# A layer stack on one core: where the attention outputs are turned, and how the branch products are cut

## The reference, cut to what matters

```python
y_fox = forgetting_attention(q_f, k_f, v_f, cum_logf).reshape(B, S, FOX_W)      # 8 heads, 512 wide
y_dsa = indexer_sparse_attention(q_d, k_d, v_d, q_i, k_i, w_i, rel_bias)        # 8 heads, 512 wide
merged = (jax.nn.sigmoid(gate_fox) * (y_fox @ w_branch_fox)
          + jax.nn.sigmoid(gate_dsa) * (y_dsa @ w_branch_dsa))
x = x + gate1 * (merged @ w_out)
```

## Time and profile before

| | |
|---|---|
| median of 3 runs | 1379.53 us (1378.36 to 1380.99) |
| profiled execution | 1380.45 us, span 1378.7 us |
| PE busy | 1329.7 us, 96% |
| PE weight loads | 1095.1 us, 79% |
| DVE busy | 824.6 us, 60% |
| ACT busy | 657.1 us, 48% |
| mean granted PE clock | 0.997 of full speed |

### The profile page before, as it was taken

One profiled execution on the slowest core, in us unless ns is written; L12 is line 12 of the kernel. 1 busy time (PEld: TensorE's weight loads), 2 busy tenths in 40 slices (PEclk: granted clock), 3 DMA queues, 4 the chain that ended last, 5 costly groups with the idle time before them and its releaser, 6 DMA issues.

```text
span 1378.7 us, 16276 instructions
## 1 busy us (share of the span) xinstructions
PE 1329.7 (96%) x6233; PEld 1095.1 (79%) x6233; DVE 824.6 (60%) x1119; ACT 657.1 (48%) x1048; POOL 79.9 (6%) x116
## 2 busy tenths in 40 slices
PE   2999999999999999999999999999999999999997
PEld 2788877788888788888877888887888888888885
DVE  5686767868465654457447554556553575755454
ACT  2666655553444543345655444444443444544342
POOL 3501100100000100001001000001000010100000
PEclk9999999999999999999999999999999999999999
DMA  9767654458455655654625754647556555564551
GB/s 336 252 201 250 233 206 173 163 183 316 142 196 170 214 184 197 195 187 172 207 111 161 218 193 161 202 164 229 183 201 196 184 194 203 184 213 184 172 203 52
DMA packets 156716, 268.37 MB, mean 195 GB/s; under 512 B 9477, under 2 KB 101717, under 8 KB 155616
## 3 DMA queue, kind: packets, MB, share of 16 engines
q1 hardware_dynamic: 148896, 239.43, 50.9%
q0 software_dynamic: 7744, 27.91, 6.0%
HBM read 266.21 MB, written 1.07 MB: 194 GB/s over the span
## 4 chain that ended last, share of the span: by engine, by line
PE 84%; DVE 5%; DMA 4%; ACT 3%; POOL 1%; issue 1%; SPq 0%; DVEq 0%; ACTq 0%; POOLq 0%
PE UP L685 16%; PE UP L687 16%; PE UP L686 16%; PE Y L685 9%; PE Y L687 9%; PE Y L686 9%; PE TB L759 3%; DVE WL L1449 2%; DMA RAW<-in_ffn_w_gu 2%; DMA RAW<-in_w_in 1%; DMA X<-in_x 1%; ACT WH L1088 1%; POOL RS L610 1%; PE Y L791 1%; POOL VAR L609 1%
## 5 line engine op out<-in xcount | busy, mean ns | idle before, releaser
L1449 DVE TENSOR_TENSOR WL<-RAW,WH 128x1024 fp32r<-128x1024 f32 (+1 forms) x442 | 507.8, 1194 | 186.0 <-ACT WH L1088 180.1
L1088 ACT CAST WH<-RAW 128x1024 fp32r<-128x1024 f32 (+1 forms) x442 | 429.9, 1032 | 220.1 <-PE Y L687 121.3
L685 PE MATMUL UP<-WH,AH 128*128 128x512 f32 (+1 forms) x1136 | 458.7, 404 | 5.1 <-DVE WL L1449 4.3
L687 PE MATMUL UP<-WH,AL 128*128 128x512 f32 (+1 forms) x1136 | 443.8, 391 | 0.0
L686 PE MATMUL UP<-WL,AH 128*128 128x512 f32 (+1 forms) x1136 | 442.6, 390 | 0.0
L685 PEld LDWEIGHTS UP<-WH,AH 128*128 128x128 f32 x1136 | 214.3, 189 | 49.6 <-issue 8.2
L687 PEld LDWEIGHTS UP<-WH,AL 128*128 128x128 f32 x1136 | 214.0, 188 | 45.3
L686 PEld LDWEIGHTS UP<-WL,AH 128*128 128x128 f32 x1136 | 214.7, 189 | 40.1 <-issue 0.2
L685 PE MATMUL Y<-WH,HH 128*128 128x512 f32 (+1 forms) x496 | 193.6, 390 | 0.0
L687 PE MATMUL Y<-WH,HL 128*128 128x512 f32 (+1 forms) x496 | 191.6, 386 | 0.0
L686 PE MATMUL Y<-WL,HH 128*128 128x512 f32 (+1 forms) x496 | 191.4, 386 | 0.0
(11 more groups left out here) (228 smaller groups left out, 932.8 us busy)
## 6 DMA issues: line engine op xcount, KB each, us to landing
RAW<-in_ffn_w_gu SPq DMA_DIRECT2D x176, 512.0 KB, 5.0
RAW<-in_ffn_w_down SPq DMA_DIRECT2D x80, 512.0 KB, 4.1
RAW<-in_w_mlp SPq DMA_DIRECT2D x64, 512.0 KB, 4.2
RAW<-in_w_in SPq DMA_DIRECT2D x38, 512.0 KB, 5.8
PIECE<-in_w_ada POOLq DMA_DIRECT2D x32, 512.0 KB, 5.4
RAW<-in_a_w_in SPq DMA_DIRECT2D x24, 512.0 KB, 4.6
WADA<-in_w_ada SPq DMA_DIRECT2D x7, 1024.0 KB, 10.0
RAW<-in_w_out SPq DMA_DIRECT2D x8, 512.0 KB, 4.1
```

Source lines behind the costliest of these rows:

```text
L685: pe.matmul(dst, ah, wh, start=first, stop=False)
L687: return pe.matmul(dst, al, wh, start=False, stop=last)
L1088: act.copy(WH[:, u % 2, q * n:(q + 1) * n], raw_half(u, q // 2)[:, (q % 2) * n:(q % 2 + 1) * n]).then_inc(wh_done, 1)
L1449: ve.tensor_tensor(WL[:, u % 2, o], raw_half(u, q // 2)[:, (q % 2) * n:(q % 2 + 1) * n], WH[:, u % 2, o].bitcast(F32), ALU.subtract).then_ ...
```

## The change

The forgetting outputs' high and low parts no longer go to AH and AL but to BH and BL, two views of HL over the old key space, which is free from head 7 on. So they can be turned while AH and AL are still read by the wide units: the turn, two ACT copies and two DVE subtractions move into unit 9. branch(1,0) and branch(1,1) are cut in two halves (two of four contraction blocks each). The first half of branch(1,0) stands ahead of slot 15, the second behind it. The row sums are made as four and two instead of three and three. The sparse outputs' turn stands between the halves of branch(1,1). ACT rounds unit 12 in two halves around outputs(15) and makes the sparse outputs' high copies ahead of all four sigmoids. DVE splits the first half of unit 12 straight behind head 15's logits and makes all six row copies behind the last reciprocal.

```diff
+        BH, BL = HL[:, 8:12, :], HL[:, 12:16, :]
...
 (PE, in the loop over units 0 to 10)
+                if u == 9:
+                    pe.wait_ge(y_done, NF)
+                    for tok in range(TOK):
+                        turn(("y", tok, 1), 4, YA[:, tok, HALF:D])
                 wide(u, 1, head=head)
...
             values(head)
-            for tok in range(TOK):
-                turn(("y", tok, 1), 4, YA[:, tok, HALF:D])
-            head = slot(2 * NF - 1, 0, 2 * NF)
-            pe.wait_ge(piece_used, PIECES)
-            for c in range(4, 7):
-                ada_sum(c, c - 4)
-            values(head)
-            def branch(b, tok, banks, turns=None):
+            def branch(b, tok, banks, turns=None, ks=None):
                 ready(("y", tok, b))
-                deep(UNIT[("br", b)], tok, AH, AL, 4 * b, True, True, f"br{b}", turns, banks)
+                ah, al, k0 = (AH, AL, 0) if b == 0 else (BH, BL, 0)
+                deep(UNIT[("br", b)], tok, ah, al, k0, True, True, f"br{b}", turns, banks, ks)
...
-            branch(1, 0, UP)
+            branch(1, 0, UP, ks=(0, 1))
+            head = slot(2 * NF - 1, 0, 2 * NF)
+            branch(1, 0, UP, ks=(2, 3))
+            values(head)
+            pe.wait_ge(piece_used, PIECES)
+            for c in range(4, 8):
+                ada_sum(c, c - 4)
             head = slot(2 * NF, 0, 2 * NF)
-            for c in range(7, 10):
+            for c in range(8, 10):
                 ada_sum(c, c - 4)
             values(head)
             pe.wait_ge(m_done, 2 * NF)
-            branch(1, 1, Y[0])
+            branch(1, 1, Y[0], ks=(0, 1))
             pe.wait_ge(y_done, 2 * NF)
             for tok in range(TOK):
                 turn(("y", tok, 0), 4, YA[:, tok, 0:HALF], FLIP)
+            branch(1, 1, Y[0], ks=(2, 3))
             branch(0, 0, Y[1])
...
 (ACT)
+                    if u == 9 and tok == 0:
+                        branch_high(1)
             outputs(head)
-            branch_high(1)
             outputs(slot(2 * NF - 1, 0, 2 * NF))
-            round_unit(UNIT[("br", 0)])
+            round_unit(UNIT[("br", 0)], (0, 1))
+            outputs(slot(2 * NF, 0, 2 * NF))
+            round_unit(UNIT[("br", 0)], (2, 3))
+            branch_high(0)
             for b in (1, 0):
                 for tok in range(TOK):
                     s = slice(2 * (1 - b), 2 * (1 - b) + 2)
                     act.activation(SIG[:, s, tok, :], SIG[:, s, tok, :], ACT.Sigmoid).then_inc(sig_done, 1)
-                if b == 1:
-                    outputs(slot(2 * NF, 0, 2 * NF))
-            branch_high(0)
...
 (DVE)
+                    if u == 9:
+                        branch_low(1)
                     modulation(1)
...
-            branch_low(1)
             slot(2 * NF - 1, 0, 2 * NF)
-            ada_out(4, 7)
             split_unit(UNIT[("br", 0)], (0, 1))
             slot(2 * NF, 0, 2 * NF)
-            ada_out(7, 10)
+            ada_out(4, 10)
             split_unit(UNIT[("br", 0)], (2, 3))
+            branch_low(0)
             weighted(1, 0, UP)
-            branch_low(0)
             weighted(1, 1, Y[0])
             split_unit(UNIT[("wout", 0)])
             weighted(0, 0, Y[1])
```

More of the change, by code:

```diff
@@ L1205, in mod_highs, with branch_high @@
                                    scale=SCALE[:, k:k + 1]).then_inc(mod_high, 1)
+            def branch_high(b):
+                dst = AH[:, 0:4, :] if b == 0 else BH
+                for tok in range(TOK):
+                    high(("y", tok, b), dst[:, :, tok * P:(tok + 1) * P], HALF)
             round_unit(0, (0, 1))
@@ L1279, in _ @@
                         att += 1
+                    if u == 9 and tok == 0:
+                        branch_high(1)
             outputs(head)
-            def branch_high(b):
-                for tok in range(TOK):
-                    high(("y", tok, b), AH[:, 4 * b:4 * b + 4, tok * P:(tok + 1) * P], HALF)
-            branch_high(1)
             outputs(slot(2 * NF - 1, 0, 2 * NF))
-            round_unit(UNIT[("br", 0)])
+            round_unit(UNIT[("br", 0)], (0, 1))
+            outputs(slot(2 * NF, 0, 2 * NF))
+            round_unit(UNIT[("br", 0)], (2, 3))
+            branch_high(0)
             for b in (1, 0):
@@ L1667, in chosen, with branch_low @@
                                  ).then_inc(sel_done, 1)
+            def branch_low(b):
+                hi, lo = (AH[:, 0:4, :], AL[:, 0:4, :]) if b == 0 else (BH, BL)
+                for tok in range(TOK):
+                    ts = slice(tok * P, (tok + 1) * P)
+                    low(("y", tok, b), lo[:, :, ts], hi[:, :, ts], HALF)
             att = 0
@@ L1708, in ada_out @@
                     plain(("ada", c), ADA[:, (c - 4) // 2, (c % 2) * HALF:(c % 2 + 1) * HALF], P, HALF)
[L1710 to L1714, removed]
             def weighted(b, tok, banks):
```

## The result

| | before | changed |
|---|---|---|
| median | 1379.64 us (1378.36 to 1380.99, 4 runs) | 1388.22 us (1386.69 to 1389.45, 4 runs) |
| ratio | | 1.0061, 95% interval 1.0048 to 1.0074 |
| profiled execution | 1380.45 us, span 1378.7 | 1388.32 us, span 1386.4 |
| PE busy | 1329.7 us | 1331.6 us |
| granted clock, mean | 0.997 | 0.995 (0.993 in the three others) |

In a second measurement, on another occasion, the ratio was 1.0048 (1.0035 to 1.0062). The forecast was 1383.4 us with a range up to 1385.6: the direction is right, the size is not.

The account below looks back on a forecast made before the run. PE was taken to bound the kernel (84% of the last chain). Waits 1.35 - 1.1 + 2.0 = +2.2 us plus one clock fall of 1.7 gave +3.9, from median 1379.53 to 1383.4 us; range 1379.6 to 1385.6.

Parts of the forecast that it names:

- Edit 1: Tenth unit: eight transposes of the forgetting outputs put in after head 11's scores cost PE 0.85 us, with no wait behind.
- Edit 2, the bank of row sum 4: PE waits 3.3 us before the third row sum for DVE's copy behind two splits; branch(1,1) starts 1.35 us late.
- Edit 3: Sparse outputs' turn between the halves of branch(1,1): no wait before branch(0,0), 1.1 us gained.
- What is late next: Turn of m inside branch(0,1): PE waits 2.0 us, because four ACT sigmoids stand ahead of w_out's rounding.
- The clock: PE's granted clock falls once, behind the 3.3 us gap before the third row sum, costing 1.7 us.
- the rival with 0.12: Two falls of PE's clock, the second behind the wait before the turn of m: +5.6 us, 1385.1 us; chance 0.12.
- Sum: Whole kernel: waits +2.2 us plus one clock fall 1.7 us make +3.9 us.
- The Trainium skill's figure: 0.8 us lost per fall of PE's clock, which would make the total +3.0 us; the forecast used 1.7 instead.

Follow-up runs that it names:

- experiment 1: Changed kernel with DVE's copies of row sums 4 to 7 ahead of the split of the sparse branch's first half; ratio 1.002 to the kernel before.
- experiment 5: Changed kernel with ACT's order alone edited: two forgetting sigmoids behind head 15's probabilities, one sparse sigmoid ahead of the high copies; ratio 1.0065 to the kernel before.
- experiment 2: Changed kernel with 16 matmuls, results unused, filling each of PE's two gaps; ratio 1.002 to the kernel before.
- experiment 10: Kernel before with only the sparse outputs' turn moved between the halves of branch(1,1); ratio 0.9989.
- experiment 7: Changed kernel with row copies and reciprocal ahead of DVE's split and POOL's row loads later, ACT's order left; ratio 1.0007 to the kernel before.
- experiment 3: Changed kernel with POOL's two row loads waiting for the turn of m instead of the sparse outputs' turn; ratio 1.0048 to the kernel before.
- experiment 4: The changed kernel run again unedited for a second profile; ratio 1.0048 to the kernel before.
- experiment 9: Kernel before with only the forgetting outputs' turn moved into the tenth unit, into the old key space; ratio 1.0006.
- experiment 6: Changed kernel with row copies and reciprocal ahead of DVE's split and ACT's sigmoids earlier, row loads left in place; ratio 1.0006 to the kernel before.
- experiment 8: Changed kernel with row copies and reciprocal ahead of DVE's split, ACT's sigmoids earlier and row loads later; 1377.08 us against 1381.22 before, ratio 0.9972.

## Why the prediction was wrong, point by point

- **Edit 1**, +0.85: measured +0.88, no wait behind it. Right.
- **Edit 2, the bank of row sum 4**, 3.3 us: measured 3.17, released by DVE's copy behind two splits. Experiments 1 and 5 confirm the path: the copy behind the split, the split behind ACT. Right. What follows it was put a little too long: from the third row sum to branch(1,1) takes 4.45 us at full clock (experiment 2), where 0.95 + 3.74 was taken, and without the slow clock branch(1,1) is 1.05 us late, not 1.35.
- **Edit 3**, -1.1: measured -1.14, and by itself in experiment 10. Right.
- **What is late next**, 2.0 us (T is the start of branch(1,1)): the term was mis-sized because its mechanism was incomplete. The sigmoids ahead of the rounding are worth a gap of 2.1 us by themselves (experiment 7, also 3), close to what was predicted (1.7, and 0.2 to 0.3 between the halves). The step that failed is "DVE's first split at T + 10.7, the fourth done 4.55 later": it took w_out's second half as landed, a wait on the load at nothing. DVE's splits of w_out in the changed kernel:

```profile
227.76 2.36 DVE L1457 TENSOR_TENSOR WL<-RAW,WH 128x1024 fp32r<-128x1024 f32 x2 [1.17 <-ACT WH L1094]
231.05 2.36 DVE L1457 TENSOR_TENSOR WL<-RAW,WH 128x1024 fp32r<-128x1024 f32 x2 [0.94 <-ACT WH L1094]
```

The first starts at T + 10.8 and the fourth is done 5.65 us later, 1.1 more than predicted, and the wait was 3.06 us (2.7 in experiment 4) instead of 1.7 and a little. Behind it is POOL's wait for the sparse outputs' turn, which the prediction nowhere has: that turn moved ahead, the split that releases w_out's second half moved back, and the two transfers met. The prediction said that POOL's queue was not reordered; that is true, and it does not follow that its transfers stay where they were.

- **The clock**, one fall of 1.7 us: this is the term that failed most. There were two falls, since the second gap came to 2.7 to 3.1 us. That was the rival with 0.12, held down by the gap of 1.7 us on which it was weighed. And a fall did not always cost what the one example in the earlier trace rows did: 1.7 us behind the first gap in one profile, 3.0 in the next, 1.5 and 1.8 behind the second. Together that is 3.2 us in the first profile and 4.8 in the second. Experiment 2 measures both falls by the time: 4 to 5.6 us, give or take about 2.
- **Sum.** In the first profile the waits came to +2.9 (0.88 + 1.86, less 1.7 for the slow clock, is 1.05; then -1.14 and +3.04), where 1.35 - 1.1 + 2.0 = 2.2 was predicted. The clock came to +3.2, where 1.7 was predicted. That makes 6.2 against 3.9. The medians differ by 8.6 us in the first measurement and by 6.7 in the second; no run places the difference between the two.
- **The Trainium skill's figure** ("TensorE: Matmul & The Clock Gate", section "HAM oscillation — how this bites in real kernels"), from which 0.8 us a fall was worked out, was too low here throughout: the cheapest fall cost 1.5 us. The 1.7 us of the earlier trace rows fits the short falls and was too low for the long one.

What stays open: why the fall behind the first gap sometimes begins within the gap and lasts twice as long. No run here tells it apart: the two profiles of the changed kernel differ in it and the kernel is the same. What the longer fall does to the whole time is open too. In the first measurement the profiled execution had the short fall and a mean clock of 0.995, and the three others 0.993, yet they took 1386.7 to 1389.5 us, around its 1388.3.

## What to carry to other kernels

When work is put between two engines to cover a wait, list for every shared buffer who frees it and what now stands ahead of that instruction in its own queue; here one copy behind one split cost 3.2 us of waiting and a fall of the clock on top. Do the same for each semaphore that a DMA queue waits on: a queue whose own order is untouched still moves when its releaser moves, and two transfers that were 4 us apart may meet. On TensorE, in work like this price a new gap of about 2 us or more at the gap plus what the clock takes behind it (1.5 to 3.0 us here), and keep both ends of that price, because it was not the same from run to run.

## What the runs showed of the hardware that was not expected

- Behind one and the same gap of 3.17 us the granted clock was at 1.2 GHz for 3.4 us in one execution (loss 1.7 us) and for 6.9 us in two others (loss 3.4 us, 0.4 to 0.5 of it within the gap).
- Sixteen matmuls whose result nobody reads, put into each gap, took the ratio from 1.0048 to 1.002, some 4 us, and the granted clock stayed at 2.4 GHz.
- A gap of 1.66 us (experiment 9) brought no fall; gaps of 2.1 and 2.6 us (experiments 3 and 7, and 6) did, and in the kernel before one of 2.15.
- A 1 MB load (two issues of 512 KB) could be used 8.9 us after its issue when it started together with two row loads of 512 KB each (8.4 to 8.9 in experiments 1, 4, 5 and 6), and 4.7 us after it when it did not (experiment 8).
